# Two tiles in turn through the scan's inverse, a finish by token, outputs rounded where they are made

## The reference

```python
y_fox = fox_attention(q, k, v, log_f)             # causal, 8 heads of 64, decay bias
yr = rwkv7_scan(rh, decay, kh, vh, -kk, kk * ah)  # st = st*w + (st a) b + v k ; y = st r
mu = jnp.mean(yr, axis=-1, keepdims=True)         # per head
var = jnp.mean(jnp.square(yr - mu), axis=-1, keepdims=True)
yr = ((yr - mu) * lax.rsqrt(var + GN_EPS)).reshape(bsz, s_len, RWKV_WIDTH)
yr = yr * gn_g[i] + gn_b[i]
y_rwkv = (yr + bonus).reshape(bsz, s_len, RWKV_WIDTH) * g
merged = gate_fox * (y_fox @ w_o_fox[i]) + gate_rwkv * (y_rwkv @ w_o_rwkv[i])
x = x + merged @ w_out[i]
x = x + (jax.nn.gelu(u[..., :D_FF], approximate=True) * u[..., D_FF:]) @ w_down[i]
ple_gate = jax.nn.sigmoid(rmsnorm(x, g_ple[i]) @ w_ple_gate[i])
x = x + ple_gate * (p[i] @ w_ple_up[i])
```

## Time and profile before

| | |
|---|---|
| median of 3 runs | 4095.05 us (4091.77 to 4100.69) |
| the profiled execution's own time | 4087.94 us |
| its span | 4085.9 us |
| busy: PE / PEld / DVE / ACT / POOL | 88% / 66% / 48% / 28% / 40% |
| mean granted TensorE clock | 0.936 |

### The profile page before, as it was taken

One profiled execution on the slowest core, in us unless ns is written; L12 is line 12 of the kernel. 1 busy time (PEld: TensorE's weight loads), 2 busy tenths in 40 slices (PEclk: granted clock), 3 DMA queues, 4 the chain that ended last, 5 costly groups with the idle time before them and its releaser, 6 DMA issues. The chain is left out here.

```text
span 4085.9 us, 58517 instructions
## 1 busy us (share of the span) xinstructions
PE 3596.3 (88%) x24988; PEld 2695.0 (66%) x24988; DVE 1956.1 (48%) x1909; ACT 1129.7 (28%) x1570; POOL 1646.2 (40%) x901
## 2 busy tenths in 40 slices
PE   5999799879899798987999987767979899999978
PEld 4887333668677333766777777644567688888857
DVE  4433565642542665633659014454552562626524
ACT  3224344421223443411345112214410210101122
POOL 1332366432333466443356434313433344444423
PEclk9999799989999899988999989977989899999989
DMA  4012100043111100032211210010032111111111
GB/s 178 31 46 74 46 1 1 15 180 140 47 40 69 20 1 14 11 150 65 87 54 65 88 63 4 4 72 1 1 129 77 47 45 49 51 48 52 47 41 67
DMA packets 93013, 226.80 MB, mean 56 GB/s; under 512 B 28240, under 2 KB 37584, under 8 KB 91744
## 3 DMA queue, kind: packets, MB, share of 16 engines
q1 hardware_dynamic: 76528, 192.94, 13.6%
q10 hardware_dynamic: 16240, 30.28, 2.3%
HBM read 184.36 MB, written 38.83 MB: 55 GB/s over the span
## 5 line engine op out<-in xcount | busy, mean ns | idle before, releaser
L1672 PE MATMUL acc<-h_hi,weights_hi 128*128 128x512 f32 (+1 forms) x928 | 365.8, 394 | 24.4 <-DVE h_lo L1830 18.4
L1673 PE MATMUL acc<-h_lo,weights_hi 128*128 128x512 f32 (+1 forms) x928 | 340.4, 367 | 0.0
L1674 PE MATMUL acc<-h_hi,weights_lo 128*128 128x512 f32 (+1 forms) x928 | 340.0, 366 | 0.0
L957 DVE TENSOR_REDUCE part_max<-aux 128x2 f32<-128x856 f32 (+5 forms) x234 | 237.9, 1017 | 210.8 <-PE aux L823 145.0
L2290 PE MATMUL acc<-h_hi,weights_hi 128*128 128x512 f32 x672 | 274.3, 408 | 25.4 <-DVE h_lo L2568 15.4
L3130 PE MATMUL acc<-h_hi,weights_hi 128*128 128x512 f32 x704 | 275.8, 392 | 13.4 <-DVE h_lo L536 9.9
L3178 POOL TENSOR_TENSOR weights_hi<-weights,ones 128x1024 fp32r<-128x1024 f32 (+1 forms) x66 | 122.7, 1860 | 392.1 <-PE acc L3132 392.1
L3131 PE MATMUL acc<-h_lo,weights_hi 128*128 128x512 f32 x704 | 275.4, 391 | 0.0
L3132 PE MATMUL acc<-h_hi,weights_lo 128*128 128x512 f32 x704 | 275.1, 391 | 0.0
L1844 DVE RECIPROCAL arena<-arena 128x512 f32<-128x512 f32 (+1 forms) x48 | 141.7, 2953 | 263.3 <-ACT arena L1807 263.3
L2292 PE MATMUL acc<-h_hi,weights_lo 128*128 128x512 f32 x672 | 263.5, 392 | 0.0
(11 more groups left out here) (433 smaller groups left out, 8482.0 us busy)
## 6 DMA issues: line engine op xcount, KB each, us to landing
weights<-in_w_in SPq DMA_DIRECT2D x44, 512.0 KB, 3.3
weights<-in_w_up SPq DMA_DIRECT2D x43, 512.0 KB, 3.3
arena<-in_w_mod SPq DMA_DIRECT2D x6, 2048.0 KB, 9.4
weights<-in_w_out SPq DMA_DIRECT2D x21, 512.0 KB, 5.2
weights<-in_w_mod SPq DMA_DIRECT2D x4, 2048.0 KB, 22.0
mixer_gates<-arena SPq DMA_DIRECT2D x32, 256.0 KB, 2.0
x_between<-arena ACTq DMA_DIRECT2D x16, 512.0 KB, 2.6
weights<-in_w_gates SPq DMA_DIRECT2D x16, 512.0 KB, 3.4
```

What stands on the lines that cost most here:

```text
L957: nc.vector.tensor_reduce(part_max[:, b % 2, j, :, i:i + 1], max_tile(m)[:, :, 0:cw], AX_X, ALU.max, negate=True).then_inc(max_done, 1)
L1672: nc.tensor.matmul(out, w_hi[:, b, k, :], hi[:, k, cols], start=(k == 0), stop=False)
L1673: nc.tensor.matmul(out, w_hi[:, b, k, :], lo[:, k, cols], start=False, stop=False)
L1674: return nc.tensor.matmul(out, w_lo[:, b, k, :], hi[:, k, cols], start=False, stop=(k == KD - 1))
```

## The change

1. **Scan.** Tiles go in pairs. The pair's two tiles take each inner step in turn, each with a PSUM region, levels, inverses and copies of its own. PE now waits at a tile's step for the copy of that tile's step just before. The 16 outer steps of the pair before are spread over the pair's 54 inner steps; the last pair's 16 stand alone at the end. `masks`, `state` and `u` move into the arena's tail, and the load of `bonus` moves to `rwkv_finish`.
2. **Finish by token.** The variance is made with the tokens on the partitions (`var`, 128x64 for everything), so root and reciprocal run once on 128x64; a matmul with a broadcast column spreads the result back into PSUM. All four centrings come first. ACT and DVE also split the result into high and low part, tile by tile.
3. **Attention.** The first pair's copies are divided: ACT makes 2, DVE makes 2 (6 with own keys). Three large clears go (two on POOL, one in `attention_operands`); the second score matmul reads 65 rows instead of 128. In the forgetting attention POOL splits the outputs of blocks 0 to 5 in two operations each, nine exponentials after the block's last; ACT and DVE split the last two at the end.
4. **Merge.** `part_tiles` for y is gone. `gemm_merge` takes the rwkv product first; `xT` is loaded in `gemm_residual`, in 8 pieces from ACT's queue.
5. **Last stage.** `load`, `part_tiles` and `gemm_store` for p are gone. `gemm_gated_residual` makes the 12 up matmuls of a tile behind its 48 gate matmuls, into PSUM that DVE multiplies from; those of tiles 0 and 1 come before the norm is ready. Weights are split with 10 blocks of columns instead of 8.

```diff
-    order = [(0, s, None) for s in inner_steps]
-    for t in range(n_tiles):
-        if t + 1 < n_tiles:
...
+    for t0 in range(0, n_tiles + 2, 2):
+        outer_steps = [(t, None, (ci, s)) for t in (t0 - 2, t0 - 1) for ci in range(2) for s in range(4)] if t0 else []
+        if t0 == n_tiles:
+            order += outer_steps
+            continue
+        done, begun = 0, 0
+        for s in inner_steps:
+            for t in (t0, t0 + 1):
+                order.append((t, s, None))
+                begun += 1
+                while done < len(outer_steps) and (done + 1) * 2 * Q <= begun * len(outer_steps):
+                    order.append(outer_steps[done])
+                    done += 1
...
                 def inner(t, s):
-                    q = t * Q + at[s]
-                    dst, out = region[q % 2], blocks[q % 2]
-                    if q >= 2:
-                        wait_used(pe, (q - 2) // Q, inner_steps[(q - 2) % Q])
+                    level_t, level, inv, inv_t, g_sb, p_sb = buffers(t)
+                    dst, out = region[t % 2], blocks[t % 2]
+                    if at[s]:
+                        wait_used(pe, t, inner_steps[at[s] - 1])
+                    elif t >= 2:
+                        wait_used(pe, t - 2, inner_steps[-1])
```

```diff
+                def variance(p):
                     pe.wait_ge(sq_ready, p + 1)
-                    for c0, cw in MAIN:
-                        mm = nc.tensor.matmul(pg.acc[:, 1, c0:c0 + cw], cn["head_mean"][:], sq[:, c0:c0 + cw], start=True, stop=True)
+                    for t in range(per_tile):
+                        i = p * per_tile + t
+                        mm = nc.tensor.matmul(var[:, 2 * i:2 * i + 2], sq[:, p % 2, t * P:(t + 1) * P], by_head, start=True, stop=True)
...
+                def spread_rstd(p):
+                    if p >= 2:
+                        pe.wait_ge(scaled, p - 1)
+                    for t in range(per_tile):
+                        for hh in range(2):
+                            one = rstd[:, p * per_tile + t, hh:hh + 1].to_broadcast([P, HD])
+                            mm = nc.tensor.matmul(pg.acc[hh * HD:(hh + 1) * HD, p % 2, t * P:(t + 1) * P], one, cn["ident"][:], start=True, stop=True)
...
+                dve.wait_ge(std_ready, 1)
+                nc.vector.reciprocal(rstd[:], rstd[:]).then_inc(inverted, 1)
```

```diff
# pair_attention: PE, then POOL
-                        pe.wait_ge(q_rounded, 4 * p + 4)
-                        if own_keys:
-                            pe.wait_ge(k_rounded, 4 * p + 4)
+                        pe.wait_ge(q_rounded, 4 * p + 2)
+                        if own_keys and p:
+                            pe.wait_ge(k_rounded, 4 * p)
+                        if p == 0:
+                            pe.wait_ge(first_copied, 6 if own_keys else 2)
...
+                    for b in part_after.get(e, ()):
+                        pool.wait_ge(divided, b + 1)
+                        nc.gpsimd.tensor_tensor(hi, out, pg.ones[:].to_broadcast([P, qn]), ALU.mult).then_inc(pool_rounded, 1)
...
+                        nc.gpsimd.tensor_tensor(lo, out, full(hi), ALU.subtract).then_inc(pool_parted, 1)
# gemm_gated_residual: PE, from tile 2 on
+                for t in range(2, n):
+                    pe.wait_ge(w.parted, t + 3)
+                    pe.wait_ge(opened, t - 1)
+                    for c0, cols in MAIN:
+                        for k in range(KD):
+                            gate_product(t, k, c0)
+                    pe.wait_ge(gated, 2 * (t - 1))
+                    up_products(t).then_inc(acc_ready, 1)
```

More of the change, by code:

```diff
@@ L788, in pair_attention @@
         spread, divided = pg.sem("spread"), pg.sem("divided")
+        first_copied, part_rounded, parted = pg.sem("first_copied"), pg.sem("part_rounded"), pg.sem("parted")
+        part_after, part_last = {}, []
+        for b, (first, last, p, q0, qn) in enumerate(blocks if parts else ()):
+            if last + 9 < len(exps):
+                part_after.setdefault(last + 9, []).append(b)
+            else:
+                part_last.append(b)
         per_exp = 2 if pairs[0].bias else 1
@@ L2077, in gemm_merge @@
-def gemm_merge(pg, w_fox, w_rwkv, y, gates_dram, merged, x_load):
+                for t in range(n):
+                    dve.wait_ge(opened, t + 1)
+                    for c in range(2):
+                        half = gate[:, t % 2, c * BANK:(c + 1) * BANK]
+                        nc.vector.tensor_tensor(half, half, ups[t % 2][c], ALU.mult).then_inc(gated, 1)
+                    dve.wait_ge(gated, 2 * t + 2)
+                    tile = x[:, t, 0:SEQ]
+                    nc.vector.tensor_tensor(tile, tile, gate[:, t % 2], ALU.add).then_inc(added, 1)
@@ new lines, in rwkv_scan @@
+    inner_at, by_dve_before, by_act_before = {}, {}, {}
+    for t, s, _ in order:
+        if s is not None:
+            inner_at[t, s] = len(inner_at)
+            by_act_before[t, s] = sum(by_act[at[k]] for _, k in inner_at)
+            by_dve_before[t, s] = len(inner_at) - by_act_before[t, s]
+    pool_order = []
+    for t0 in range(0, n_tiles, 2):
+        for j in range(LEVELS):
+            pool_order += [(t, j, True) for t in (t0, t0 + 1) if j < LEVELS - 1] + [(t, j, False) for t in (t0, t0 + 1)]
@@ L3053, in _ @@
+                act.wait_ge(var_ready, R_TILES)
+                nc.scalar.activation(rstd[:].rearrange("p t h -> p (t h)"), var, ACT.Sqrt, bias=eps[:]).then_inc(std_ready, 1)
+                for p in range(R_TILES):
+                    act.wait_ge(done, p + 1)
+                    nc.scalar.copy(hi[:, p, :], bonus[:, p, :]).then_inc(y_rounded, 1)
             @block.vector
             def _(dve):
-                step = Counter(dve, own)
                 tt, stt = nc.vector.tensor_tensor, nc.vector.scalar_tensor_tensor
@@ L3066, in _ @@
[L3066 to L3072 removed]
+                    dve.wait_ge(spread, p + 1)
@@ L3076, in _ @@
[L3076 to L3077 removed]
+                    if p:
+                        low(p - 1)
+                low(R_TILES - 1)
+                dve.wait_ge(c_parted, 1)
+                dve.wait_ge(y_parted, R_TILES)
 def feed_forward(pg, cn, x, h, conv, conv_b, g, maker_in):
@@ L3297, in second_block @@
         gated.close()
[L3298 to L3306 removed]
+        norm = lambda u, rstd_all: Norm(pg, cn, xT, h, gain("g_ple_2"), u, rstd_all)
+        gemm_gated_residual(pg, weight_tiles(I["w_ple_gate_2"]), weight_tiles(I["w_ple_up_2"]), I["p_2"], h, xT, pg.out, norm)
 def scale_columns(pg, cols, by):
```

434 lines of the change are left out of this document (253 added, 181 removed).

## The result

Median 4064.35 us beside 4097.58 us for the kernel before: a ratio of 0.9933, 95% interval 0.9915 to 0.9951. One of the changed kernel's four executions took 6805.24 us, for a reason that no run shows; it counts in the median but not in the ratio, and the other three lie between 4059.79 and 4066.23. The changed kernel is faster by 0.67%, some 27 us (the medians alone differ by 33). I had forecast 55.5 us less, 4039 us, with a range of 4010 to 4064. The direction is right, the size is half of the forecast, and the median lies 0.35 us outside the range. Without the long execution the median is 4062.47, just inside it.

What follows compares the result with a forecast made beforehand. No engine was taken as full, so latency counts, with PE's issue stalls in the scan. Scan -20, finish -11, forgetting attention -9, first attentions -2, `w_out` +1, last stage -14.5 sum to -55.5: 4039 us, range 4010 to 4064.

Steps and rivals of the forecast that it cites:

- First layers' attentions: Two attentions, each with two of its four first copies of 1.04 us moved to DVE: -1 each, -2 us.
- The clears cost nothing either way: Forgetting attention: removing the clears gains 0, since POOL's were done under the copies.
- Forgetting attention and parts: `part_tiles` gone -10.8, earlier start -2, POOL's sixth block +2.3, last two blocks on ACT and DVE +1.4: -9 us.
- Scan: Paired tiles hide PE's wait for the same tile's steps; steady pair 62 us, first 48; 275.3 us in all, -20.
- Stalls that are not waits for data are not filled by a second tile: Scan pairs: the "issue" stalls of two tiles, 6.7 us, stay in each pair's time.
- rival A: Scan: the stalls go with the pairs, a pair takes 54 us, scan -47, in all 4013 us; chance 0.2.
- 55.4 + 6.7: Scan's steady pair: PE's own work for two tiles plus their issue stalls, taken as 62 us.
- Finish: `rwkv_finish`: four reciprocals of 26.2 us become one of 0.4; stage 49.6 us, -11 (0 to -14).
- Merge and `w_out`: Merge in the other order 0; `w_out` +1 us (0 to +3), as x's eight pieces meet the first weights' load.
- Last stage: 36.80 us of small stages removed, 22.2 added for up matmuls, later norm and wider weight splits: -14.5 us.
- B: Scan pairs gain nothing (68.6 to 69.8 us); only other stages save, 4060 to 4067 us; chance 0.2.

Runs made afterwards that it cites:

- Experiment 2: Kernel before with one line changed: second score product reads 65 rows instead of 128, clears kept; 4110.86 us, ratio 1.0062 to the kernel before.
- experiment 4: Changed kernel with 128 rows in the second score product and POOL's clears begun only after the first copies; 4035.20 us, ratio 0.9888 to the kernel before.
- experiment 3: Changed kernel with the forgetting attention's outputs split in a stage of their own behind it; 4054.18 us, ratio 0.9931 to the kernel before.
- experiment 5: Changed kernel with 8 matmuls of 128 columns for 16 of 64 in 21 of a tile's 27 inner scan steps, numbers wrong; 4021.16 us.
- experiment 7: Changed kernel with 8 more already-satisfied semaphore waits ahead of each inner scan step from the second pair on; 4072.50 us.
- combined versions: Changed kernel with 128 rows, late clears and reordered lone chunks, with or without merged level 0 identity products; 4019.21 and 4025.49 us, ratios 0.9836 and 0.9843.

## Why the prediction was right or wrong

By stage, the profile lost 25.2 us of the 55.5 forecast. The stages below miss by 14.5, 8.2, 12.6, -5.6, 1.8 and 0.7 us, and all others together took 1.9 less.

**First layers' attentions, forecast -2, measured +12.5.** The step that failed. Its own mechanism was right: divided copies bring the first maximum forward, 2.5 us in the first attention (I had 1, from copies of 1.04 us; these have 1280 columns and take 1.26). But "The clears cost nothing either way" passed over why they could go: the product reads 65 rows. I costed the edit's instructions and took matmuls of the same columns for the same price, and put no term for it. Each matmul does take the same, 0.63 us at half clock; what changes is how long the half clock is granted. Experiment 2 prices it at 26 us in all in the kernel before, and experiment 4 gives back 23 in the changed one. That this is about the whole gap between forecast and result is in part chance, since the scan's miss and the finish's gain lie on either side.

**Forgetting attention and parts, -9, measured -0.8.** The stage of 10.7 went. The start came sooner as forecast. The parts cost 5.3 instead of 3.7, and the rows some 6 that I didn't have; the split is no better than experiment 3 has it.

**Scan, -20, measured -7.4.** The structure was right: 3.6 for the masks, a first pair of 49.5 (48), four lone chunks of 9.4 us. The term mis-sized is the steady pair: 62 forecast, 63.2 and 66.4 measured, and about 67 for the last up to its lone chunks: some 11 us in three pairs. "Stalls that are not waits for data are not filled by a second tile" was right, and rival A (54) was refuted by the time; 54 came out only with a third of the records gone. Both terms of 55.4 + 6.7 were off, and one was missing. In the mean pair of 64.8 us, PE was busy 51.2 at full clock; the waits of "issue" were 8.5, more than the stalls of two lone tiles; and some 4.5 were waits for copies, which I had put at nothing. With a third of the matmuls gone (experiment 5) PE is busy 47.4, "issue" is 0, and the waits for copies are 6.5. The rule of the Trainium skill, "Runtime: NRT & Kernel Launch", section "Instruction fetch mechanics", that fetching is mostly hidden isn't refuted: what held PE was not shown to be the fetching, but the handling of instructions, of which experiment 7 has the price.

**Finish, -11, measured -16.6.** Right, and better than forecast. Here is the one reciprocal, and the first scaling behind the spreading:

```profile
2722.04 0.55 DVE L3228 RECIPROCAL rstd<-rstd 128x64 f32<-128x64 f32 x1 [3.13 <-ACT rstd L3208]
2726.49 1.28 DVE L3234 SCALAR_TENSOR_TENSOR arena<-arena,gn_g,acc 128x1024 f32<-128x1024 f32 x1 [3.90 <-PE acc L3181]
```

The reciprocal was done after 19.2 us, not 24.7: the mean products and the variances (1.84 for 16 records) ran at full clock from the stage's fifth microsecond on, where I took the stage's mean clock of before. From the first scaling on it took 20.9 us (22.5 forecast). The first spreading took longer, 3.9 us up to the scaling instead of 2.9.

**Merge and `w_out`, +1, measured +2.8,** inside its bound. **Last stage, -14.5, measured -13.8.** Right in its terms but one: the tiles take 2.72 us more each, the first tile's gate comes 4.5 later (4.6 forecast), and POOL's wider split costs 2.4 where I had 1.0 (2.32 and 3.90 us for a tile instead of 1.90 and 2.40).

**The rivals.** B named the result's size (4060 to 4067) by luck: its mechanism, a pair of 68.6 to 69.8 us, was not what happened; pairs gained, and attentions lost. That the time came so near the end of the range is the same luck, since the range reached so far for B's sake. No rival held that an edit costed at nothing could lower TensorE's clock. The direction was right.

## What to carry to other kernels

Where a kernel is bound by TensorE and runs in part at half clock, as this one does, an edit that leaves the matmuls' number and columns alone isn't free: look at the granted clock of the stretch, and measure an edit to the contracted rows by itself. Where steps are many small matmuls, count TensorE's instructions, waits among them, before adding a second stream to fill its gaps. And ask of each operation that a change removes what it was in the way of: here a clear of 4 us that hid under ACT's copies blocked VectorE's.

## What the runs showed of the hardware

- Rows of zeros count. Contracting over 65 rows instead of 128, with no other difference, cost 26 us (ratio 1.0062). The matmul took 0.63 us at half clock either way, but the first attention spent 89 us at half clock instead of 55. In the first attention of all profiled executions it was 57 to 89 us with 65 rows and 40 to 59 with 128. That the rows lower the clock is shown; by what rule is not.
- A VectorE rounding copy of 0.82 us took 5.00 under a POOL clear of 4.36, and ended 0.68 after it.
- A wait for a count long reached cost 22 ns in TensorE's queue (432 of them made a pair 9.5 us longer).
- The same four chunks took 7.7 us each in one execution at half clock and 5.2 in another at full clock, 10 us in one stage. The combined versions' times, 4009 to 4025 and 4019 to 4041 us, are the longer the lower their mean granted clock (0.950 to 0.944 and 0.947 to 0.940); whether it is the scan's end that decides it was not tested.

Still open: how much of the forgetting attention's time is where the low clock happens to end, and what within TensorE's sequencing costs the time of an instruction.
